# Depthwise convolution of a decoder trunk: fewer, true fp32 taps on TensorE, added into by VectorE

## The reference

```python
def conformer_conv_module(x, w_in, b_in, w_dw, b_dw, ln_g, ln_b, w_out, b_out):
    h = x @ w_in + b_in
    a, gate = jnp.split(h, 2, axis=-1)
    h = a * jax.nn.sigmoid(gate)
    h = causal_depthwise_conv(h, w_dw, b_dw)
    h = jax.nn.silu(layer_norm(h, ln_g, ln_b))
    return h @ w_out + b_out
```

## Time and profile before

| | us |
|---|---|
| median of 3 runs | 1038.56 (1035.69 to 1039.14) |
| the profiled execution | 1036.58 |
| its span, first to last instruction | 1034.6 |
| TensorE matmuls busy | 1022.5 (99%), 4799 |
| VectorE busy | 812.4 (79%), 1163 instructions |
| ScalarE busy | 513.0 (50%), 773 |
| GpSimd busy, without DMA issues | 233.9 (23%), 286 |
| granted TensorE clock, mean | 0.999 of full speed |

### The profile page before, as it was taken

One profiled execution on the slowest core, in us unless ns is written; L12 is line 12 of the kernel. 1 busy time (PEld: TensorE's weight loads), 2 busy tenths in 40 slices (PEclk: granted clock), 3 DMA queues, 4 the chain that ended last, 5 costly groups with the idle time before them and its releaser, 6 DMA issues.

```text
span 1034.6 us, 14305 instructions
## 1 busy us (share of the span) xinstructions
PE 1022.5 (99%) x4799; PEld 854.8 (83%) x4799; DVE 812.4 (79%) x1163; ACT 513.0 (50%) x773; POOL 233.9 (23%) x286
## 2 busy tenths in 40 slices
...
GB/s 336 169 161 154 91 120 311 227 245 278 229 254 203 84 101 101 82 284 203 186 183 183 140 102 107 305 159 269 282 232 248 168 81 101 101 82 264 203 190 115
DMA packets 65003, 189.70 MB, mean 183 GB/s; under 512 B 7488, under 2 KB 8512, under 8 KB 64960
## 3 DMA queue, kind: packets, MB, share of 16 engines
...
...
## 4 chain that ended last, share of the span: by engine, by line
PE 92%; DVE 4%; DMA 1%; issue 1%; ACT 1%; SPq 1%; POOL 0%; DVEq 0%; POOLq 0%; ACTq 0%
PE ps L1608 19%; PE ps L1610 19%; PE ps L1609 19%; PE ps L1851 6%; PE ps L1849 6%; PE ps L1850 6%; PE ps L1618 4%; PE ps L1620 4%; PE ps L1619 4%; DMA raw<-d_weights 1%; PE ps L1779 1%; DVE ps L1114 1%; PE ps L1700 1%; PE ps L1701 1%; PE ps L1699 1%
## 5 line engine op out<-in xcount | busy, mean ns | idle before, releaser
L1608 PE MATMUL ps<-xh,wh 128*128 128x512 f32 x816 | 317.7, 389 | 0.3 <-DVE wl L1045 0.3
L1609 PE MATMUL ps<-xl,wh 128*128 128x512 f32 x816 | 317.5, 389 | 0.0
L1610 PE MATMUL ps<-xh,wl 128*128 128x512 f32 x816 | 317.5, 389 | 0.0
L1608 PEld LDWEIGHTS ps<-xh,wh 128*128 128x128 f32 x816 | 153.2, 188 | 32.3 <-DVE wl L1045 0.8
L1610 PEld LDWEIGHTS ps<-xh,wl 128*128 128x128 f32 x816 | 153.2, 188 | 32.0
L1609 PEld LDWEIGHTS ps<-xl,wh 128*128 128x128 f32 x816 | 153.2, 188 | 31.8
L674 ACT ACTIVATE wh<-raw 128x1024 fp32r<-128x1024 f32 x114 | 119.9, 1056 | 81.7 <-PE ps L1851 63.4
L1045 DVE TENSOR_TENSOR wl<-raw,wh 128x1024 fp32r<-128x1024 f32 x101 | 122.9, 1222 | 41.9 <-ACT wh L674 41.9
L528 POOL TENSOR_SCALAR veps<-sqs 128x1 f32<-128x1 f32 x15 | 5.7, 380 | 554.1 <-ACT squares L849 554.1
L1341 DVE TENSOR_TENSOR wl<-raw,wh 128x1024 fp32r<-128x1024 f32 x80 | 97.6, 1220 | 7.7 <-ACT wh L903 7.6
L1851 PE MATMUL ps<-wh,parts 128*128 128x512 f32 x264 | 102.7, 389 | 0.0
...
...
## 6 DMA issues: line engine op xcount, KB each, us to landing
...
```

The costliest lines, as they stand in the source:

```text
L1608: eng.matmul(ps[:, bank, cols], a, xh[:, k, cols], start=(k == 0), stop=False)
L1609: eng.matmul(ps[:, bank, cols], a, xl[:, k, cols], start=False, stop=False)
L1610: mm = eng.matmul(ps[:, bank, cols], b, xh[:, k, cols], start=False, stop=(k == KD - 1))
```

## The change

In tiles 0 to 6 the work on the 31 taps is divided anew.

- **TensorE** has no taps in tile 0 and three in tiles 1 to 5, eight in tile 6 as before. A tap is now one matmul with true fp32 operands (`glu` itself and a diagonal `diagf`) instead of three with split ones. `gluh`, `glul`, `diagh` and `diagl` are left for tile 7 alone.
- TensorE's taps come first in a tile, and **VectorE** goes on in TensorE's bank (`CHAIN`, 4 or 5): in tiles 1 to 5 its even taps from tap 2 on are added into it, which waits for TensorE's taps (`dw_pe`) at tap 2. VectorE's other bank is `SUMS[j % 2]`, begun by **ScalarE** (`begun`, tap 0 written straight to PSUM, semaphore `own_ok`). In tile 0 ScalarE begins both banks. In tile 6 VectorE's two banks are 6 and 1 (`SIXTH`), both begun by ScalarE, and TensorE's is apart as before.
- VectorE's end of a tile is one add (`close_sum`) and, after the next tile's first tap, one scalar_tensor_tensor with the bias into `cbuf` (`close_chain`). The next tile's gate comes two taps before the tile's end, instead of after it.
- TensorE takes a third unit before tile 1's taps, and then per tile: three taps, a unit, the transposes of the tile before, a unit.
- **GpSimd** starts the low parts of units 8 to 15 in pairs, one transfer of 1 MB for two units, and those of units 5 and 6 during tile 0.

VectorE's taps (taps of a tile, tile by tile): before 17 in each; after 20, 18, 18, 18, 18, 18, 15.

```diff
-PE_TAPS = [5, 5, 5, 5, 5, 5, 8] + [20]
+CHAINED = KD - 2
+PE_TAPS = [0] + [3] * (CHAINED - 1) + [8] + [20]
 GP_TAPS = [9, 9, 9, 9, 9, 9, 6]
...
-LAST_AT = 11
-UNIT_4_AT = 10
-POOL_TILES = 2
+LAST_AT = 8
+UNIT_4_AT = 5
...
+LO_DMAS = [[LEAD + 2], [LEAD + 3], [LEAD + 4]] + [[u, u + 1] for u in range(LEAD + 5, U_CONV_OUT, 2)] + [[U_CONV_OUT], [U_CONV_OUT + 1]]
+LO_DMA = {u: d for d in LO_DMAS for u in d}
...
+    CHAIN = (4, 5)
+    SIXTH = (6, 1)
...
```

On GpSimd:

```diff
         def lo(u):
-            eng.wait_ge(w_neg, u - BY_DMA[0] + 1)
-            eng.dma_start(split_at(u)[1], raw[:, u % RAW, :], accum_op=ALU.add).then_inc(lo_in[u % RAW], 16)
+            n, slot, q = len(LO_DMA[u]), u % RAW, u % RING
+            eng.wait_ge(w_neg, u + n - BY_DMA[0])
+            eng.dma_start(wl[:, q:q + n, :], raw[:, slot:slot + n, :], accum_op=ALU.add).then_inc(lo_in[slot], 16)
...
-        diagonals(0, 0, PE_TAPS[0])
-        add_products(0, range(1, AT_ONCE))
-        diagonals(1, 0, PE_TAPS[1])
-        add_products(0, range(AT_ONCE, GP_TAPS[0]))
+        eng.affine_select(out=diagf[1][:, 0:n, :], in_=w, compare_op=ALU.is_equal, fill=0.0,
+                          base=0, pattern=[[0, n], [-1, P]], channel_multiplier=1).then_inc(diag_p, 1)
+        add_products(0, range(1, 4))
+        lo(LEAD + 2)
+        add_products(0, range(4, 6))
+        lo(LEAD + 3)
+        add_products(0, range(6, GP_TAPS[0]))
...
         for j in range(1, KD):
-            for u in (2 * j + LEAD, 2 * j + 1 + LEAD):
-                if u in BY_DMA and u < BY_DMA[-1]:
-                    lo(u)
             if j < KD - 1:
+                lo(2 * j + LEAD + 1 if j > 1 else LEAD + 4)
                 add_products(j, range(1, GP_TAPS[j]))
...
```

On ScalarE:

```diff
+        def begun(j, k, bank):
+            if j >= 2:
+                eng.wait_ge(conv_c, j - 1)
+            c = C_CDW_W + j * TAPS + k
+            eng.activation(ps[:, bank, :], glu[:, j % 2, k:k + SEQ], ACT.Copy, scale=par[:, c:c + 1]).then_inc(own_ok, 1)
...
-            eng.activation(gluh[:, j % 2, PAD:CW], glu[:, j % 2, PAD:CW], ACT.Copy).then_inc(glu_hi, 1)
...
+        for j in range(1, CHAINED):
             eng.wait_ge(glu_s, j + 1)
+            begun(j, 0, SUMS[j % 2])
+            products(j, 0, 4)
             if j >= 2:
                 ct_out(j - 2)
+            products(j, 4, 6)
...
+            if j + 1 < CHAINED:
+                diagonals(j + 1, range(PE_TAPS[j + 1]))
...
+            products(j, 6, GP_TAPS[j] - 1)
+            sigmoid(j + 1)
+            his([2 * j + LEAD + 3])
+            products(j, GP_TAPS[j] - 1, GP_TAPS[j])
+            if j + 1 < CHAINED:
+                his([2 * j + LEAD + 4])
...
```

On VectorE:

```diff
+        def chain_of(j):
+            if j == 0:
+                return [(k, SUMS[0] if k % 2 else CHAIN[0]) for k in [3] + [k + d for k in range(2, DV_TAPS[0] - 2, 2) for d in (3, 0)] + [DV_TAPS[0] - 2]]
+            if j == CHAINED:
+                return [(k, SIXTH[k % 2]) for k in range(2, DV_TAPS[j])]
+            return [(k, SUMS[j % 2] if k % 2 else CHAIN[j % 2]) for k in range(1, DV_TAPS[j])]
+        def close_sum(j):
+            bank = SUMS[j % 2]
+            eng.wait_ge(dw_tap, ended[j, bank])
             eng.wait_ge(gp_add, adds_before(j + 1))
+            return stat(eng.tensor_tensor(gsum[:, j % 2, :], ps[:, bank, :], gsum[:, j % 2, :], ALU.add))
+        def close_chain(j, n):
...
+            eng.scalar_tensor_tensor(out=cbuf[:, j % 2, :], in0=gsum[:, j % 2, :], scalar=par[:, c:c + 1],
+                                     in1=ps[:, bank, :], op0=ALU.add, op1=ALU.add).then_inc(conv_c, 1)
+        gated_channels(0)
+        los([LEAD])
...
+        for j in range(CHAINED + 1):
+            chain = chain_of(j)
+            for i, (k, bank) in enumerate(chain):
...
+                if j < CHAINED and i == len(chain) - 2:
+                    gated_channels(j + 1)
...
+                if (j, bank) in ended:
+                    eng.wait_ge(dw_tap, ended[j, bank])
+                elif 0 < j < CHAINED and bank == CHAIN[j % 2]:
+                    eng.wait_ge(dw_pe, j)
+                else:
+                    eng.wait_ge(own_ok, begun_of.get((j, bank), j + 2))
+                eng.wait_ge(glu_s, j + 1)
+                eng.scalar_tensor_tensor(out=ps[:, bank, :], in0=glu[:, j % 2, k:k + SEQ], scalar=par[:, c:c + 1],
+                                         in1=ps[:, bank, :], op0=ALU.mult, op1=ALU.add).then_inc(dw_tap, 1)
...
+                if j > 0 and i == 0:
+                    close_chain(j - 1, n)
+            if j < CHAINED:
+                n = close_sum(j)
...
```

On TensorE:

```diff
-        def taps(j, amid=None):
+        def first_taps(j):
...
             for q in range(n):
...
-                eng.matmul(ps[:, 4 + b, :], diagh[b][:, q, :], gluh[:, b, k:k + SEQ], start=(q == 0), stop=False)
-                eng.matmul(ps[:, 4 + b, :], diagh[b][:, q, :], glul[:, b, k:k + SEQ], start=False, stop=False)
-                mm = eng.matmul(ps[:, 4 + b, :], diagl[b][:, q, :], gluh[:, b, k:k + SEQ], start=False, stop=(q == n - 1))
+                mm = eng.matmul(ps[:, CHAIN[b], :], diagf[b][:, q, :], glu[:, b, k:k + SEQ],
+                                start=(q == 0), stop=(q == n - 1))
             mm.then_inc(dw_pe, 1)
...
-        for j in range(1, KD):
-            unit_conv(2 * j)
-            if j in (1, KD - 1):
-                unit_conv(2 * j + 1)
-            if j >= 2:
-                to_tm(j - 2)
-            taps(j - 1)
-            if 1 < j < KD - 1:
-                unit_conv(2 * j + 1)
+        unit_conv(2)
+        unit_conv(3)
+        unit_conv(4)
+        for j in range(1, CHAINED):
+            first_taps(j)
+            unit_conv(2 * j + 3)
+            to_tm(j - 1)
+            unit_conv(2 * j + 4)
+        unit_conv(2 * KD - 1)
+        first_taps(CHAINED)
+        to_tm(CHAINED - 1)
```

More of the change, by code:

```diff
@@ L218, in build_trunk @@
     dwl = place("dwl", [P, KD * TAPS], f32)
[L219 to L221 removed]
+    diagf = [place(f"diagf{b}", [P, max(PE_TAPS[b:KD - 1:2]), P], f32) for b in range(2)]
+    diagh = place("diagh", [P, PE_TAPS[KD - 1], P], f32r, h0)
+    diagl = place("diagl", [P, PE_TAPS[KD - 1], P], f32r)
     ctm = place("ctm", [P, NT, D], f32)
@@ L412, in lo_of @@
         if u in BY_DMA:
-            return lo_in[u % RAW], 16 * ((u - BY_DMA[0]) // RAW + 1)
+            slot = LO_DMA[u][0] % RAW
+            return lo_in[slot], 16 * sum(d[0] % RAW == slot and d[0] <= u for d in LO_DMAS)
         return w_lo, u + 1 - (len(BY_DMA) if u >= BY_DMA[0] else 0)
@@ L799, in _ @@
                 eng.activation(brow[:, :], brow[:, :], ACT.Copy, scale=1.0 / ALPHA).then_inc(bo1_ok, 1)
[L800 to L812 removed]
+            if j + 1 < CHAINED:
+                diagonals(j + 1, range(PE_TAPS[j + 1]))
+            else:
+                diagonals(j + 1, range(PE_TAPS[j + 1] // 2))
+            products(j, 6, GP_TAPS[j] - 1)
[4 more added lines that the diff above has]
+                his([2 * j + LEAD + 4])
+            else:
+                diagonals(j + 1, range(PE_TAPS[j + 1] // 2, PE_TAPS[j + 1]))
+                diagonals(j + 2, range(sum(POOL_LAST), PE_TAPS[j + 2] - 1))
+        j = CHAINED
+        eng.wait_ge(glu_s, j + 1)
+        begun(j, 0, SIXTH[0])
+        products(j, 0, 2)
+        begun(j, 1, SIXTH[1])
+        products(j, 2, 3)
+        ct_out(j - 2)
+        products(j, 3, AT_ONCE)
+        diagonals(j + 1, range(PE_TAPS[KD - 1] - 1, PE_TAPS[KD - 1]))
+        sigmoid(KD - 1)
+        products(j, AT_ONCE, GP_TAPS[j])
         eng.wait_ge(glu_s, KD)
[L814 removed]
         eng.activation(gluh[:, 1, PAD:CW], glu[:, 1, PAD:CW], ACT.Copy).then_inc(glu_hi, 1)
@@ L1130, in _ @@
+        def close_chain(j, n):
+            bank = CHAIN[j % 2]
+            c = C_CDW_B + j
+            eng.wait_ge(dw_tap, ended[j, bank])
+            eng.wait_ge(st_ok, n)
             if j >= 2:
                 eng.wait_ge(ct_pe, j - 1)
-            eng.tensor_tensor(cbuf[:, j % 2, :], gsum[:, j % 2, :], pe_bank, ALU.add).then_inc(conv_c, 1)
+            eng.scalar_tensor_tensor(out=cbuf[:, j % 2, :], in0=gsum[:, j % 2, :], scalar=par[:, c:c + 1],
+                                     in1=ps[:, bank, :], op0=ALU.add, op1=ALU.add).then_inc(conv_c, 1)
```

155 lines of the change are left out of this document (59 added, 96 removed).

## The result

The changed kernel takes 1031.59 us (median of 4 runs, 1030.74 to 1032.32), the kernel before in the same comparison 1038.11 (4 runs): ratio 0.994, 95% interval 0.9921 to 0.996. On four later occasions the kernel before had medians of 1036.97 (20 runs), 1037.15 (17), 1037.42 (9) and 1036.75 (9); the changed kernel, run again beside the third, had 1031.89 (5 runs, ratio 0.9948, interval 0.9935 to 0.9962). So the gain is about 5.5 us; the forecast was 4.4 and 1034.2. Of the 2.3 to 2.6 us between 1034.2 and the two medians, 1.1 to 1.8 come from where the forecast started: the 1038.56 of three runs lay that far above the later medians of the kernel before. The rest is a gain that was forecast too small. The profiled execution took 1031.41 us, its span is 1029.6 (before 1036.58 and 1034.6).

A forecast was written before the change was run, and what follows sets the result against it. TensorE and VectorE were taken as bounds at once. TensorE's stage of 106.3 us becomes 76.4 + 21.6 + 2.9 + 0.5 + 0.5 = 101.9, 4.4 less: median 1034.2, range from 0.8 below the 1031.8 cap to 1038.0.

The forecast's parts named there:

- the cap by VectorE: Tiles 0 to 6: however cheap the fp32 matmul, VectorE's 6.8 us saving limits the gain, at 1031.8.
- The price of the fp32 matmul: TensorE's taps, tiles 1 to 6: 0.94 us each, so 23 take 21.6 in place of 26.8.
- the first rival: TensorE's taps: the fp32 matmul is cheaper, 0.88 us; tile 14.1, gain 5.7, 1032.8; chance 0.18.
- the switches: TensorE, between taps and other matmuls: first matmul after each kind late once more, five places at 0.1, 0.5 us.
- The wait for `glu`: TensorE before tile 1's taps: reaches them at 34.3, VectorE writes `glu` at 34.8, so 0.5 us.
- The estimate of 1.37: TensorE's fp32 taps: four 107 ns weight loads in view make t 1.37, 5.5 us slower than before, 1044.
- VectorE's sum: VectorE, tiles 0 to 6: start 36.7, five tiles of 13.76, tile 6 of 13.9; ends at 119.4 against 126.2.
- The smaller of the two savings: Convolution stage: TensorE saves 4.4 us, VectorE alone 6.8; the gain was taken as TensorE's 4.4.
- the forecast's own case: Whole kernel: t of 0.90 to 1.0, gain 3 to 5.3 us, 1033.3 to 1035.6; chance 0.45.
- GpSimd and the pairs: GpSimd's tile 13.5 us; one issue per pair saves 0.87; bytes land 7.2 after issue, 1.2 to spare, cost nothing.
- the rival about late pairs: Tiles 2 to 5: a pair lands 1 us or more late, TensorE waits, gain about 1, 1037.5; chance 0.08.
- The early gate: VectorE's gate two taps before the tile's end: 5 us to spare for TensorE, so the wait doesn't feed itself.

The follow-up runs named there:

- one_of_three: Changed kernel with TensorE doing only the first of its three taps in tiles 1 to 5, the two others left out: 1030.84 us, ratio 0.9937.
- low_part_late: Changed kernel with VectorE's subtraction for the low part of tile 7's `glu` moved behind tile 6's last tap: 1032.8 us, ratio 0.9962.
- no_pairs: Changed kernel with the low parts of units 8 to 15 as transfers of one unit each: 1031.65 us, ratio 0.9946.
- late_gate: Changed kernel with the next tile's gate product behind the tile's last two taps instead of ahead of them: 1038.7 us, ratio 1.0016.

## Why the prediction came out as it did

- **The two bounds** were right, and that the change must lighten both. So were the mechanism on TensorE (fp32 products in place of three each, and fewer of them), ScalarE's sum (12.0 for about 12) and the cap by VectorE as such, though not its size. The measured 1031.59 lies inside the range, near its lower end.
- **The price of the fp32 matmul was the mis-sized term.** I took 0.94, four times the 0.234 of a tap's product; it is 0.86 (6.86/8 = 0.857). Over 23 taps that is 1.9 us, and TensorE's tile is 13.99, not 14.32. This is the first rival (0.88, a gain of 5.7, at most VectorE's), which I had given 0.18. TensorE reached tile 7 at 117.42 for 119.8: of these 2.4 us 1.9 are the price, 0.1 the earlier start, and 0.4 lie in the switches, for which the sum had 0.5. The wait for `glu` came as forecast: three units of 5.46 from 17.79 end at 34.17, the taps start at 34.71, so 0.54 for 0.5 (the row's 0.31 counts from the modelled end of the last matmul). The four passes of the Trainium skill (FP8 and Floating Point Precision, section TensorE Precision Notes) fit 0.86, which is 4 x 512 columns at the 2.4 GHz level (0.853); the records show two matmuls, so passes can't be counted in them. That fast weight load is off for fp32 (TensorE: Matmul & The Clock Gate, section Weight-path perf modes) cost nothing here: 0.188 of load, not the 0.107 of the estimate, lies beside 0.43 of matmul. The estimate of 1.37 worked out from that page is refuted.
- **VectorE's sum** held for tile 1 (13.76 forecast and measured; begun at 36.62 for 36.7), but it ended tile 6 at 120.63 for 119.4. Tiles 1 to 5 were 69.37 for 68.8: 0.1 to 0.2 of waiting for TensorE in each of tiles 3 to 5, where I had 0.5 (in `one_of_three`, with less on TensorE, the step is 0.66 again). Tile 6 was 120.63 - 105.99 = 14.64 for 13.9: the low part of `glu` cost 1.15 where I counted 0.6, because it now falls beside a running add of GpSimd; the other 0.2 are short stalls ahead of the last two adds. I had moved that instruction and not asked who is busy at its new place. The Trainium skill (SBUF — State Buffer, section SBUF: two separate sides) has a VectorE operation with two SBUF inputs and a GpSimd operation that reads SBUF exclude each other for a whole instruction; `low_part_late` agrees, 1.15 beside the add and 0.60 without it.
- **The smaller of the two savings** was to be TensorE's 4.4. It became VectorE's: counted from the first sigmoid tile 6 ended at 108.05 before (126.21) and at 102.76 after, 5.3 less, and TensorE waits 0.59 for it. So I was low by 0.9, the price of the matmul less what VectorE's end gave back; the forecast's own case reached to just that gain, 5.3, though with t down to 0.90 and not with 0.86.
- **GpSimd and the pairs**: right in the issue (0.86 for 0.87), near in the landing (7.5 for 7.2), and no unit waited for a pair, so the rival about late pairs didn't come up. GpSimd's tile was 13.9 for 13.5, since it waits 0.4 to 0.9 for ScalarE's products. The pairs are worth 0.6 to 0.7 us at the end in the trace of `no_pairs`, through ScalarE's product buffers and not through the wait of VectorE that I had looked for; the medians don't show it.
- **The early gate** I had only as 5 us to spare for TensorE. Undoing it costs more than the whole gain (`late_gate`), since the taps of TensorE are then behind VectorE's gate and ahead of VectorE's second tap in one loop.
- **The tail**: forecast as unchanged, and nearly so. Of 5.2 us at the second projection 4.7 to 4.8 are left at the end. The traces place the loss at two waits of TensorE for VectorE. The first matmul that waits for `xl` comes 4.99 earlier than before (138.09 for 143.37, less the first sigmoids), and the first transposes of `res` 4.64 earlier (172.03 for 176.96), with a wait of 0.72 where there was one of 0.41. Why VectorE is not earlier there isn't shown.
